# Strassen's seven products for the gate and up products of 18 FFN blocks

## What is computed

```python
def swiglu_ffn(x, gain, w_gate, w_up, w_down):
    h = rms_norm(x, gain)
    return (jax.nn.silu(h @ w_gate) * (h @ w_up)) @ w_down
...
x = x + 0.5 * swiglu_ffn(x, ffn1_norm[l], ffn1_w_gate[l], ffn1_w_up[l], ffn1_w_down[l])
...
x = x + 0.5 * swiglu_ffn(x, ffn2_norm[l], ffn2_w_gate[l], ffn2_w_up[l], ffn2_w_down[l])
```

## Time and profile before

| | us |
|---|---|
| median of 3 runs | 1034.03 |
| lowest, highest | 1031.8, 1711.59 |
| span of the profiled execution | 1029.8 |
| PE, DVE, POOL, ACT busy in it | 1020.8, 545.6, 386.1, 367.5 |

### The profile page before, as it was taken

How to read it: one execution, slowest core, us unless ns; L and a number is a source line. 1 busy time by engine, 2 the same in 40 slices (tenths; PEclk the granted TensorE clock), 3 DMA queues, 4 the chain that set the end, 5 groups by cost and what they waited for, 6 DMA issues and landing times.

```text
span 1029.8 us, 14318 instructions
## 1 busy us (share of the span) xinstructions
PE 1020.8 (99%) x5674; PEld 841.4 (82%) x5674; DVE 545.6 (53%) x839; ACT 367.5 (36%) x503; POOL 386.1 (37%) x97
## 2 busy tenths in 40 slices
PE   9999999999999999999999999999999999999998
PEld 7878888888888888788877888888888888888887
DVE  5593344433444477862557884784333443344435
ACT  7533213222132243444356664632321322213220
POOL 0164433434434431533252201526353443443440
PEclk9999999999999999999999999999999999999999
DMA  8333222232232221231221001313323223222212
GB/s 320 126 123 122 82 101 103 81 119 85 81 118 86 89 115 41 88 117 41 83 78 48 3 2 41 123 41 123 123 81 116 87 81 122 81 88 116 81 41 82
DMA packets 15734, 94.80 MB, mean 92 GB/s; under 512 B 2000, under 2 KB 2128, under 8 KB 5456
## 3 DMA queue, kind: packets, MB, share of 16 engines
q1 hardware_dynamic: 15696, 94.27, 25.4%
HBM read 92.16 MB, written 2.10 MB: 92 GB/s over the span
## 4 chain that ended last, share of the span: by engine, by line
PE 91%; DVE 4%; DMA 1%; issue 1%; ACT 1%; POOL 1%; SPq 1%; POOLq 0%; DVEq 0%
PE bank L1497 83%; DMA raw<-stream 1%; POOL wlo L387 1%; PE bank L1851 0%; DVE prob L1255 0%; PE bank L1855 0%; DVE rowmax L1257 0%; PE bank L1899 0%; ACT sqx L477 0%; DVE alo L874 0%; PE bank L1782 0%; PE bank L1965 0%; PE bank L1877 0%; PE bank L1801 0%; PE bank L1954 0%
## 5 line engine op out<-in xcount | busy, mean ns | idle before, releaser
L387 POOL TENSOR_TENSOR wlo<-raw,whi 128x2048 fp32r<-128x2048 f32 x80 | 370.1, 4629 | 548.0 <-ACT whi L452 534.7
L1497 PE MATMUL bank<-ahi,whi 128*128 128x512 f32 x944 | 370.6, 393 | 2.2 <-POOL wlo L387 2.2
L1497 PE MATMUL bank<-ahi,wlo 128*128 128x512 f32 x944 | 367.7, 389 | 0.0
L1497 PE MATMUL bank<-alo,whi 128*128 128x512 f32 x944 | 367.4, 389 | 0.0
L452 ACT ACTIVATE whi<-raw 128x2048 fp32r<-128x2048 f32 x80 | 152.6, 1912 | 339.9 <-PE bank L1497 315.9
L1497 PEld LDWEIGHTS bank<-ahi,whi 128*128 128x128 f32 x944 | 177.2, 188 | 42.5 <-POOL wlo L387 2.6
L1497 PEld LDWEIGHTS bank<-ahi,wlo 128*128 128x128 f32 x944 | 177.2, 188 | 37.1
L1497 PEld LDWEIGHTS bank<-alo,whi 128*128 128x128 f32 x944 | 177.3, 188 | 35.9
L1017 DVE SCALAR_TENSOR_TENSOR x<-bank,x 128x512 f32<-128x512 f32 x176 | 120.9, 690 | 83.8 <-PE bank L1497 83.2
L1497 PE MATMUL bank<-hhi,whi 128*128 128x512 f32 x352 | 137.2, 390 | 0.0
L1497 PE MATMUL bank<-hlo,whi 128*128 128x512 f32 x352 | 137.0, 389 | 0.0
(11 more groups left out here) (277 smaller groups left out, 739.1 us busy)
## 6 DMA issues: line engine op xcount, KB each, us to landing
raw<-stream SPq DMA_DIRECT2D x80, 1024.0 KB, 4.7
raw<-stream SPq DMA_DIRECT2D x6, 512.0 KB, 6.5
x<-x_in SPq DMA_DIRECT2D x4, 512.0 KB, 7.2
out<-x SPq DMA_DIRECT2D x8, 256.0 KB, 2.0
raw<-stream SPq DMA_DIRECT2D x4, 256.0 KB, 6.5
memx<-mem_in SPq DMA_DIRECT2D x2, 512.0 KB, 10.6
cst<-const_in SPq DMA_DIRECT2D x1, 480.0 KB, 7.3
cst<-const_in SPq DMA_DIRECT2D x1, 256.0 KB, 5.7
```

The source lines that it names most:

```text
L387: nc.gpsimd.tensor_tensor(wlo[:, u % RING, :], raw[:, u % RAW, :], whi[:, u % RING, :].bitcast(F32), ALU.subtract).then_inc(w_lo, 1)
L1497: ins = E.matmul(dst, a, b, start=(n == 0 and i == 0), stop=(n == last and i == 2))
```

## The change

Blocks 2 to 10 of each FFN (FAST = 9, twice, so 18 "bodies") compute gate and up by Strassen's algorithm. The contraction (1024) is cut into two halves, the 256 output columns into two halves of 128, the 512 tokens into two halves of 256. A gate or up block is then seven products of 4 x 3 matmuls with 256 columns, in place of 16 x 3 with 512 columns (`seventh`). Blocks 0 and 1 and all down products keep their form.

- **Operands of x.** x is normalised first (`normalize`: x times gain times rbc, 8 instructions on DVE), so that no scaling by rbc follows. Seven operands of 128 x 1024 columns per FFN, T_B11, T_1, T_3, T_2, T_B21, T_4, T_B22: three are blocks of x, four are differences (`t_total`, DVE); high parts by ACT (`t_high`), low parts by DVE (`t_low`), that of T_2 by POOL. This is done once per FFN, next to blocks 0 and 1.
- **Operands of the weights.** Per body and for each of gate and up DVE makes four sums of pieces (128 x 512) in three instructions of 1024, 512 and 512 columns (`weight_sums`). ACT writes the high parts of 14 pieces and of the down unit (`pieces_high`), POOL the low parts of the 14 pieces, one by one (`piece_low`), DVE those of the down unit (`down_low`). The ring has the same size, counted in 12 slots of one piece; a body needs 18.
- **Results.** PE does four products of gate, four of up, three of gate, three of up, then down of the block before. Between the fourth and fifth product ACT copies a quarter (`p6_copy`) and DVE combines in three instructions (`combine`); after the seventh DVE corrects two quarters (`fix`). Silu reads the bank directly.
- **Loads.** SP loads the body's units when POOL is done with the last piece of the same kind of the body before (count 11 of 14 for gate, 14 for up), and the down unit after `down_low`.
- The loops over blocks are unrolled. `mem_sums` and the memory's copies now come before the hidden products of block 0.

The diff, cut (`...`); not shown are the placing of buffers, the counters of the weight splits outside the bodies, and the host's order of the weights:

```diff
+HALF = T // 2
+K2 = KD // 2
+PIECE = 512
+SLOTS = RING * 4
+FAST = FG - 2
+BODY = 18
+POOLED = 14
+USED = BODY * FAST + 3
+(T_B11, T_1, T_3, T_2, T_B21, T_4, T_B22) = range(7)
...
+            def ffn_units(f):
+                for i in range(FAST):
+                    for g in range(2):
+                        if i == 0:
+                            sp.wait_ge(w_lo, U_SECOND[f] + 2 + g)
+                        else:
+                            sp.wait_ge(f_lo, POOLED * (FAST * f + i - 1) + (11, 14)[g])
+                        fast(f, i, g)
+                    if i > 0:
+                        sp.wait_ge(f_down_lo, (FAST + 1) * f + i)
+                    elif f == 0:
+                        sp.wait_ge(t_lo, 6)
+                    fast(f, i, 2)
...
+            def piece_low(f, i, q):
+                g = (0, 0, 0, 0, 1, 1, 1, 1, 0, 0, 0, 1, 1, 1)[q]
...
+                for ring_at, n in places(pos, 1):
+                    nc.gpsimd.tensor_tensor(in_ring(wlo, ring_at, n), whole[:, PIECE * at:PIECE * (at + 1)],
+                                            in_ring(whi, ring_at, n).bitcast(F32), ALU.subtract).then_inc(f_lo, 1)
+            def ffn_low(f):
+                for i in range(FAST):
+                    for q in range(POOLED):
+                        piece_low(f, i, q)
+                        if i == 0 and q == 3:
+                            pool.wait_ge(t_hi, 7 * f + T_2 + 1)
+                            pool.wait_ge(t_sum, 4 * f + 4)
+                            nc.gpsimd.tensor_tensor(tt[f][T_2][1][:], t_source(f, T_2), tt[f][T_2][0][:].bitcast(F32),
+                                                    ALU.subtract).then_inc(t2_lo, 1)
...
+            def ffn_bodies(f):
+                for i in range(FAST):
+                    if i == 0:
+                        pieces_high(f, 0, 8, 2)
+                    pieces_high(f, i, 10, 1)
+                    pieces_high(f, i, 11, 2)
+                    pieces_high(f, i, 13, 1)
+                    p6_copy(f, i, 0)
+                    pieces_high(f, i, 14, 4)
+                    if i < FAST - 1:
+                        pieces_high(f, i + 1, 0, 1)
+                    p6_copy(f, i, 1)
+                    fast_silu(f, i, 0)
+                    if i < FAST - 1:
+                        pieces_high(f, i + 1, 1, 3)
+                    fast_silu(f, i, 1)
+                    if i < FAST - 1:
+                        pieces_high(f, i + 1, 4, 1)
+                        pieces_high(f, i + 1, 5, 3)
+                    else:
+                        pieces_high(f, FAST, 0, 4)
+                    fast_hidden_high(f, i)
+                    if i < FAST - 1:
+                        pieces_high(f, i + 1, 8, 2)
...
+            def weight_sums(f, i, g):
+                r, s_ = raw_of(f, g), sums[f][g]
+                dve.wait_ge(fast_in[g], 16 * (FAST * f + i + 1))
+                if i > 0:
+                    dve.wait_ge(f_lo, POOLED * (FAST * f + i - 1) + (11, 14)[g])
+                elif g == 1:
+                    dve.wait_ge(t_lo, 6 * f + 3)
+                    dve.wait_ge(t_sum, 4 * f + 3)
+                link(V.tensor_tensor(s_[:, 0:2 * PIECE], r[:, PIECE:3 * PIECE], r[:, 2 * PIECE:4 * PIECE], ALU.add))
+                V.tensor_tensor(s_[:, 2 * PIECE:3 * PIECE], s_[:, 0:PIECE], r[:, 3 * PIECE:4 * PIECE],
+                                ALU.add).then_inc(s_ready, 1)
+                dve.wait_ge(s_ready, 4 * (FAST * f + i) + 2 * g + 1)
+                V.tensor_tensor(s_[:, 3 * PIECE:4 * PIECE], s_[:, 2 * PIECE:3 * PIECE], r[:, 0:PIECE],
+                                ALU.add).then_inc(s_ready, 1)
+            def down_low(f, i):
+                dve.wait_ge(f_hi, (BODY * FAST + 4) * f + BODY * i + (BODY if i < FAST else 4))
+                c0 = 0
+                for ring_at, m in places(BODY * i + (14 if i < FAST else 0), 4):
+                    ins = V.tensor_tensor(in_ring(wlo, ring_at, m), raw_down[f][:, c0:c0 + m],
+                                          in_ring(whi, ring_at, m).bitcast(F32), ALU.subtract)
+                    c0 += m
+                ins.then_inc(f_down_lo, 1)
+            def combine(f, i, g):
+                n = 2 * (FAST * f + i) + g
+                xb, yb = psum[2 * g], psum[2 * g + 1]
+                dve.wait_ge(p6_sb, n + 1)
+                link(V.tensor_tensor(u2[:, g, :], p6[:, g, :], xb[:, 0:HALF], ALU.subtract))
+                link(V.tensor_tensor(p6[:, g, :], u2[:, g, :], yb[:, 0:HALF], ALU.subtract))
+                V.tensor_tensor(xb[:, HALF:T], yb[:, HALF:T], p6[:, g, :], ALU.add).then_inc(c22_done, 1)
+            def fix(f, i, g):
+                n = 2 * (FAST * f + i) + g
+                yb = psum[2 * g + 1]
+                dve.wait_ge(y_bank_done, n + 1)
+                V.tensor_tensor(yb[:, 0:HALF], yb[:, 0:HALF], u2[:, g, :], ALU.subtract)
+                V.tensor_tensor(yb[:, HALF:T], yb[:, HALF:T], u2[:, g, :], ALU.add).then_inc(y_fixed, 1)
+            def fast_hidden(f, i):
+                n = 2 * FG * f + 2 * (i + 2)
+                for e in range(2):
+                    dve.wait_ge(silu_done, n + e + 1)
+                    if e == 0:
+                        dve.wait_ge(x_bank_done, 2 * (FAST * f + i) + 2)
+                    else:
+                        dve.wait_ge(y_fixed, 2 * (FAST * f + i) + 2)
+                    V.tensor_tensor(gbuf[:, e, :], psum[2 + e][:], gbuf[:, e, :], ALU.mult).then_inc(h_done, 1)
+                for e in range(2):
+                    dve.wait_ge(h_hi, n + e + 1)
+                    V.tensor_tensor(quarters(hlo, i % 2, e), two(e), quarters(hhi, i % 2, e).bitcast(F32),
                                     ALU.subtract).then_inc(h_lo, 1)
...
+                d0 = KD * FG * f
+                gate_scale(f, 0)
...
+                hidden(f, 0)
+                normalize(f)
+                t_total(f, T_1)
+                t_total(f, T_3)
+                t_low(f, T_B11)
+                gate_scale(f, 1)
+                t_low(f, T_1)
+                t_low(f, T_3)
+                weight_sums(f, 0, 0)
+                hidden(f, 1)
+                t_total(f, T_2)
+                for d in range(K2):
+                    ffn_add(d0, d)
+                t_total(f, T_4)
+                for d in range(K2, KD):
+                    ffn_add(d0, d)
+                weight_sums(f, 0, 1)
+                for j in (T_B21, T_4, T_B22):
+                    t_low(f, j)
+                for i in range(FAST):
+                    combine(f, i, 0)
+                    if i < FAST - 1:
+                        weight_sums(f, i + 1, 0)
+                    combine(f, i, 1)
+                    down_low(f, i)
+                    fix(f, i, 0)
+                    if i < FAST - 1:
+                        weight_sums(f, i + 1, 1)
+                    fix(f, i, 1)
+                    fast_hidden(f, i)
+                    if i == FAST - 1:
+                        down_low(f, FAST)
+                    for d in range(KD):
+                        ffn_add(d0 + KD * (i + 1), d)
...
-            def down(u, b, free, last=False):
+            def down(u, b, free):
                 for d in range(KD):
-                    if d >= 4 or last:
-                        pe.wait_ge(x_added, free + (d - 3))
+                    if free + d - 3 > 0:
+                        pe.wait_ge(x_added, free + d - 3)
...
+            def seventh(f, i, q, j, bank, h, start, fresh, done=None):
+                pe.wait_ge(f_lo, POOLED * (FAST * f + i) + q + 1)
+                if i == 0:
+                    if j == T_2:
+                        pe.wait_ge(t2_lo, f + 1)
+                    else:
+                        pe.wait_ge(t_lo, 6 * f + (j if j > T_2 else j + 1))
+                (at, _), = places(BODY * i + q, 1)
+                hi, lo, _ = tt[f][j]
+                for k in range(K2):
+                    w = tuple(in_ring(part, at + k * P, P) for part in (whi, wlo))
+                    for m, (a, b) in enumerate(((w[0], hi), (w[0], lo), (w[1], hi))):
+                        ins = E.matmul(psum[bank][:, HALF * h:HALF * (h + 1)], a, b[:, k, :],
+                                       start=start and k == 0 and m == 0, stop=k == K2 - 1 and m == 2,
+                                       skip_group_check=True)
+                        if k == 0 and m == 0:
+                            ins.then_inc(f_used, 2 if fresh else 1)
+                if done is not None:
+                    ins.then_inc(done, 1)
+            def first_four(f, i, g):
+                q, xb, yb = 4 * g, 2 * g, 2 * g + 1
+                seventh(f, i, q, T_B11, xb, 0, True, g == 0 and i > 0)
+                seventh(f, i, q + 1, T_1, yb, 0, True, False)
+                seventh(f, i, q + 2, T_3, yb, 1, False, False)
+                seventh(f, i, q + 3, T_2, xb, 1, False, False, four_done)
+            def last_three(f, i, g):
+                q, xb, yb = 8 + 3 * g, 2 * g, 2 * g + 1
```

(30 more changed lines are left out.)

381 lines of the change are left out of this document (264 added, 117 removed).

## The result

| | us |
|---|---|
| before, median of 4 runs | 1032.91 |
| after, median of 4 runs | 1083.20 |
| ratio, 95% interval | 1.0484, 1.0471 to 1.0497 |
| span of the profiled execution, before and after | 1029.8, 1081.7 |

The ratio is that of the fast runs; one of the four runs before took 1711.59 us and is not among them.

What follows compares the result with a forecast made beforehand. PE, busy 1020.8 of 1029.8 us, was taken to bound the kernel. Steady bodies -5.7, ways into the bodies +15.6 and first bodies +20.2 sum to +30: span 1060, median 1064 us; own range 1050 to 1080, over rivals 1018 to 1090.

Steps and rivals of the forecast that it cites:

- The steady stall: Steady bodies: PE waits 1.75 us before down's fifth tile (d=4) for the first add; body 32.25 us, 14 give -5.7.
- The products: Gate and up matmuls of 256 columns in the bodies: 0.1168 us each, a product of 12 matmuls 1.40 us.
- the upper bound: Spacing of 256-column matmuls: at most 0.1202 us, that of the 264-column ones in the trace.
- Rival 4: Body products: weight loads bind at 0.1296 us a matmul and the products gain nothing; chance 0.17 together with Rival 3.
- The way into FFN 1: First down of FFN 1: PE waits 12.7 us for the first add, done at 84.0; net 10.5 us later.
- a stall of 2.3: First down of FFN 1 without any POOL wait: first add at 73.7, stall paid back by 2.2 us gained earlier.
- The first bodies: First body of each FFN: late gate load delays combine(1) to 23.1; body ends at 42.8, 10.1 us more, twice, +20.2.
- The clock in all: PE's matmuls throughout: priced at full granted clock, 0.2268 us for 512 columns, with no slower matmuls after waits.
- The end of FFN 1: Last body of each FFN: 32.6 us, nothing gained or lost; the last down behind it was not looked at.
- Rival 1: Bodies after the first: PE-bound, the alternation fits into slack, all 16 take 30.5 us; 1036 us; chance 0.25.
- Rival 3: Steady bodies: whole handovers between DVE and POOL, 33.5 to 34 us a body, +21, 1086 us; chance 0.17 with Rival 4.
- the 4.2 us: Whole kernel: the profile's span lies 4.2 us below the median, so 1060 us of span became 1064 us.

Runs made afterwards that it cites:

- e1: Against the change as made: in each body the first three adds of down stand ahead of hidden's two low parts on DVE; 1047.47 us, ratio 1.0139.
- e2: Against the change as made: POOL computes only 16 of 512 columns of each piece's low part, leaving work out; 1032.05 us, ratio 0.9992.
- e6: Against the change as made: each of the seven products streams 128 of its 256 columns, leaving work out; 1081.13 us (one run), ratio 1.046.
- e4: Against the change as made: in each FFN's first body the next gate sums stand behind combine(1), down's low part and fix(0) on DVE; 1081.42 us, ratio 1.0469.
- e8: As e4, and in the first body ACT copies p6 before turning the next body's first gate piece; 1078.10 us, ratio 1.0447.
- e5: Against the change as made: behind FFN 1 DVE does all eight last-down adds before the eight low parts for the input projection; 1080.34 us, ratio 1.0455.
- e9: Against the change as made: joins e1 and e5 with a new DVE and ACT order in prelude and first body (as e8); 1043.20 us, ratio 1.0091.
- e10: Against e9: second body's next gate sums behind combine(1), their first high part behind p6_copy; prelude's first add ahead of T_1, T_2 earlier; 1042.09 us, ratio 1.0088.

## Why the forecast was right, and where it was too small

- **The steady stall.** Right in its place and its cause. Measured as the forecast did, by the matmuls, it is 2.05 us in one body and 1.22 in the next, 1.69 in the mean, where 1.75 was forecast. The shorter kind of body is the forecast's nearly instruction by instruction: the up sums end 21.3 us after its start (21.3 forecast), the low parts 26.0 (25.95), PE goes on at 26.7 (26.8), and the body takes 32.28 (32.25). The step that was too small is the one that lets POOL take a piece before the up sums begin. That holds in every second body only. In the others ACT's three pieces come in one instruction, POOL starts 0.9 us later and the first sum is caught as well; these bodies are 0.85 us longer, eight times, 6.8 us. By e1 and e2 the stall goes with either of its two conditions.
- **The products.** A term that was mis-sized, by 168 x 0.0031 = 0.52 us a body: 0.1168 taken, 0.1200 measured, which is the upper bound that was named. It does not explain the missing time, though, and here the forecast had luck: while a body waits for the adds, PE that comes to d=4 half a microsecond later waits that much less. e6 shows the same from the other side, 1.44 us less in the products and 0.1 less in the body. The term counts where PE sets the pace: in e1 a body takes 31.06 us, not 30.5. The line was drawn through 264 and 512 columns; 512, 264, 256 and 128 columns give 0.2268, 0.1202, 0.1200 and 0.1114. Rival 4 (0.1296) was wrong, but its thought was right: something that does not shrink with the columns begins to count at 256.
- **The way into FFN 1.** DVE's order in time was right nearly instruction by instruction: normalize to 65.9 (65.8 forecast), the sums to 76.3 (76.2), hidden(1) to 82.0 (82.1), the first add at 83.8 (84.0). What was missing is the 2.2 us at the lower clock after the wait. The sentence that it would be 73.7 without POOL, a stall of 2.3, does not follow from the terms beside it: 84.0 less 4.5 for normalize and 2.0 for hidden(1) is 77.5, a stall of 6. e2 with its estimate of about 5 agrees with that.
- **The first bodies.** The wait for `combine` was forecast at 7.8 and is 7.9, with the right cause (e4 and e8). PE starts d=4 at 37.7 and 37.6 us after the start of the body, where the forecast has 42.8 - 5.4 = 37.4: the longer products and some 2 us of slower matmuls behind the first wait were taken out of the stall at the adds, forecast at 4.4, of which 2.2 are left. What turns 42.8 into 44.8 is nearly all the second stretch of slower matmuls, 1.7 us behind the adds.
- **The clock in all.** Slower matmuls follow the waits at the two first downs (2.2 and 1.7 us), in the two first bodies (3.7 each, of which 1.7 reach the time) and at the end of FFN 1 (2.2 of its 7.0). So of the 22 us that were missing some 9 are the clock; the others are mainly the second handover (6.8) and the wait at the end of FFN 1 (4.8). The forecast had the clock at full speed throughout, since the earlier trace rows show nothing else; but in before PE never waits for another engine longer than 2.2 us, and the change made waits of 5 to 12.
- **The end of FFN 1.** The forecast stopped at the last body and set the last down to nothing, without a reason; it costs 7.0 us. The step not taken: to ask, at the seam, when the ring gives a slot to the next unit. In the kernel before it did so when PE started the last down (ACT at 373.48, 0.5 us after); now it does so at the fifth tile, 5.9 us after. e5 shows that this is the cause.
- **The rivals.** Rival 1 (1036 us, PE-bound bodies) is what e1 brings about in the bodies, and e1 lies 11 us above it for the other terms. Rival 3's number, 1086, is near the result, but it is the span, without the 4.2 us that the forecast adds for the median; with them it is 1091, outside the range. Its mechanism is not the one seen either: only every second body has one more handover.

## What to carry to other kernels

Fewer matmul columns for more vector work pays only if the start of the loop is counted as carefully as its steady state: here 18 bodies gain 29 us at the very best, and the lag of DVE and POOL in two starts, with the slower matmuls that it brings, costs 38 against PE alone (96.7 and 87.4 against 73.0 twice) even in the best order found. In a chain of several engines, a wait that is moved and returns tells that the work ahead of it is late, not ill placed. Moving instructions helps where the waiting one needs nothing of what stands in front of it and what is put behind it is not needed soon after (e1, three lines, 36 us). And a long wait of PE should be priced with the slower matmuls that follow it.

No order tried beats the kernel before; e9 and e10, which can't be told apart, are 0.9% slower than it (by their intervals 0.7 to 1.1%) and 3.7 to 3.8% faster than the change as made.
